# A two-layer decoder step on one core: the first and the last stage moved into the feed-forward blocks beside them

## The reference

```python
def rmsnorm(x, g):
    xf = x.astype(jnp.float32)
    y = xf * lax.rsqrt(jnp.mean(xf * xf, axis=-1, keepdims=True) + RMS_EPS)
    return y.astype(x.dtype) * g

def swiglu(h, w_in, w_out):
    gu = h @ w_in
    return (jax.nn.silu(gu[..., :D_FF]) * gu[..., D_FF:]) @ w_out
...
x += 0.5*SwiGLU(rms(x)); x += mixer(rms(x)); x += 0.5*SwiGLU(rms(x))
```

## Time and profile before

| what | value |
|---|---|
| median of 3 runs | 2402.17 us (2398.2 to 2403.61) |
| the profiled execution's own time | 2401.8 us |
| its span in the trace | 2400.0 us |
| PE busy | 2278.6 us (95%) |
| DVE, ACT, POOL busy | 1081.9, 737.5, 334.2 us |
| mean granted TensorE clock | 0.974 |

### The profile page before, as it was taken

One profiled execution on the slowest core, in us unless ns is written; L12 is line 12 of the kernel. 1 busy time (PEld: TensorE's weight loads), 2 busy tenths in 40 slices (PEclk: granted clock), 3 DMA queues, 4 the chain that ended last, 5 costly groups with the idle time before them and its releaser, 6 DMA issues. The chain is left out here.

```text
span 2400.0 us, 42964 instructions
## 1 busy us (share of the span) xinstructions
PE 2278.6 (95%) x17146; PEld 2057.5 (86%) x17146; DVE 1081.9 (45%) x1907; ACT 737.5 (31%) x1224; POOL 334.2 (14%) x422
## 2 busy tenths in 40 slices
PE   5999999996899999999999999999998889999997
PEld 5999999775764479999999999999665479999997
DVE  5442443223267644433434442444376735433433
ACT  2221332223146533322222221322255523322221
POOL 1000003100135321000012000003174320000002
PEclk8999999997999999999999999999999989999998
DMA  3332332224430022333232333332213022232331
GB/s 99 96 101 81 90 97 78 82 79 125 159 115 1 27 68 84 95 97 88 87 102 75 95 96 88 89 100 71 79 53 109 1 70 79 88 105 79 87 101 58
DMA packets 328119, 202.53 MB, mean 84 GB/s; under 512 B 11698, under 2 KB 307946, under 8 KB 327962
## 3 DMA queue, kind: packets, MB, share of 16 engines
q1 hardware_dynamic: 323866, 199.19, 27.9%
q10 hardware_dynamic: 4160, 2.10, 0.3%
HBM read 194.74 MB, written 10.70 MB: 86 GB/s over the span
## 5 line engine op out<-in xcount | busy, mean ns | idle before, releaser
L159 DVE TENSOR_TENSOR w_lo<-w_stage,w_hi 128x1024 fp32r<-128x1024 f32 (+1 forms) x268 | 356.4, 1330 | 827.1 <-ACT w_hi L152 827.0
L152 ACT ACTIVATE w_hi<-w_stage 128x1024 fp32r<-128x1024 f32 (+1 forms) x278 | 314.0, 1130 | 751.0 <-PE y_ps L166 344.2
L164 PE MATMUL gate_ps<-h_hi,w_hi 128*128 128x260 f32 x1408 | 402.3, 286 | 17.2 <-DVE h_lo L188 7.5
L165 PE MATMUL gate_ps<-h_lo,w_hi 128*128 128x260 f32 x1408 | 401.1, 285 | 0.0
L166 PE MATMUL gate_ps<-h_hi,w_lo 128*128 128x260 f32 x1408 | 400.3, 284 | 0.0
L164 PE MATMUL up_ps<-h_hi,w_hi 128*128 128x260 f32 x1408 | 398.8, 283 | 0.0
L164 PE MATMUL y_ps<-a_hi,w_hi 128*128 128x260 f32 x1408 | 398.5, 283 | 0.0
L165 PE MATMUL up_ps<-h_lo,w_hi 128*128 128x260 f32 x1408 | 398.1, 283 | 0.0
L165 PE MATMUL y_ps<-a_lo,w_hi 128*128 128x260 f32 x1408 | 398.0, 283 | 0.0
L166 PE MATMUL y_ps<-a_hi,w_lo 128*128 128x260 f32 x1408 | 397.9, 283 | 0.0
L166 PE MATMUL up_ps<-h_hi,w_lo 128*128 128x260 f32 x1408 | 397.4, 282 | 0.0
(11 more groups left out here) (420 smaller groups left out, 3142.4 us busy)
## 6 DMA issues: line engine op xcount, KB each, us to landing
w_stage<-w_ffn_in SPq DMA_DIRECT2D x176, 512.0 KB, 3.7
w_stage<-w_ffn_out SPq DMA_DIRECT2D x64, 704.0 KB, 4.5
w_stage<-w_nsa_in SPq DMA_DIRECT2D x20, 512.0 KB, 3.4
w_stage<-w_dsa_in SPq DMA_DIRECT2D x16, 512.0 KB, 3.6
w_stage<-w_nsa_out SPq DMA_DIRECT2D x8, 512.0 KB, 3.6
cmp_page<-cache_nsa_cmp SPq DMA_DIRECT2D x16, 256.0 KB, 4.3
w_stage<-w_dsa_out SPq DMA_DIRECT2D x8, 512.0 KB, 3.7
nsa_win_s<-state_nsa_win SPq DMA_DIRECT2D x1, 4080.0 KB
```

The lines of the kernel that those rows point to most:

```text
L152: act.activation(e.w_hi[slot][:, 0:cols], e.w_stage[slot][:, 0:cols], ACT.Copy).then_inc(e.hi_done, 1)
L159: dve.tensor_tensor(e.w_lo[slot][:, 0:cols], e.w_stage[slot][:, 0:cols], e.w_hi[slot][:, 0:cols].bitcast(F32), ALU.subtract).then_inc(e.lo ...
L164: pe.matmul(out, w_hi, x_hi, start=first, stop=False)
L165: pe.matmul(out, w_hi, x_lo, start=False, stop=False)
```

## The change

- `start_stage` and `final_stage` go. Two classes, `Start` and `Finish`, put their work into the streams of `ffn` 0 and `ffn` 3.
- **Start, loads**: the identity comes first, as the first 128 columns of the constants, then `x` in four loads of 128 tokens, each with its own semaphore, with the small loads between the second and third; the rest of the constants comes after weight unit 0.
- **Start, turning**: by token tile. Four transposes fill a bank with half a tile, DVE copies it into four chunks of `e.x` at once.
- **Start, norm**: ACT squares the token rows as they lie, 1024 elements each, and accumulates a sum for each token in a column (`start_sumsq`, 128 x 5). Root and reciprocal are taken on 128 x 5. DVE multiplies the identity by the factors (`rs_diag`), and in the middle of unit 1 PE multiplies it by ones, which spreads the factors over all partitions; DVE copies them to `e.rs`.
- **Start, rest**: `h_hi` no longer waits for a block's end, the two casts (`ident_b`, `causal_b`) move behind the `w_lo` of unit 2, POOL does only three memsets.
- **Finish**: ACT makes `y` as `x` times the gain, without the norm factor, as each chunk is ready (`y_of`), between the weight splits of `ffn` 3. A root of `eps` ahead of the last chunk makes the table of roots current. After the last product PE turns 7 of 8 chunks of three token tiles, then takes the sums of squares as columns (128 x 5; the last chunk's squares come from DVE as a second operand), then turns the rest. DVE and ACT copy one half of each tile each, and multiply by the factor of the token there.

The diff, cut to its core:

```diff
+class Start:
+    def sync(self, sp):
...
+        sp.dma_start(e.const[:, 0:P], e.c_const[:, 0:P]).then_inc(e.ident_landed, 16)
+        for t in range(2):
+            sp.dma_start(rows[:, t, :], xp[:, t, :]).then_inc(e.x_landed[t], 16)
+        sp.dma_start(rows[0:TS, 4, :], e.x_sample.rearrange("b s d -> (b s) d")).then_inc(e.start_loaded, 16)
+        sp.dma_start(gains[0:6 * KC, :], e.norm_g.rearrange("l s (k p) -> (l s k) p", p=P)).then_inc(e.start_loaded, 16)
+        sp.dma_start(gains[6 * KC:7 * KC, :], e.final_norm_g.rearrange("(k p) -> k p", p=P)).then_inc(e.start_loaded, 16)
+        for t in range(2, 4):
+            sp.dma_start(rows[:, t, :], xp[:, t, :]).then_inc(e.x_landed[t], 16)
+        load_units(e, sp, 0, 1)
+        sp.dma_start(e.const[:, P:], e.c_const[:, P:]).then_inc(e.const_landed, 16)
+        sp.dma_start(e.table[:, :], e.page_table.rearrange("(o b) n -> o (b n)", o=1)).then_inc(e.const_landed, 16)
+        load_units(e, sp, 1, 2)
...
+    def turns(self, pe):
+        e, rows = self.e, self.rows
+        pe.wait_ge(e.ident_landed, 16)
+        for t in range(4):
+            pe.wait_ge(e.x_landed[t], 16)
+            for i in (2 * t, 2 * t + 1):
+                if i >= 4:
+                    pe.wait_ge(e.x_done, i - 3)
+                for k in range(4):
+                    at = (i % 2 * 4 + k) * P
+                    m = pe.transpose(self.bank(i)[:, k * P:(k + 1) * P], rows[:, t, at:at + P], e.ident[:, :])
+                m.then_inc(e.turned, 1)
...
+    def spread_rs(self, pe):
+        e = self.e
+        pe.wait_ge(e.const_landed, 32)
+        pe.wait_ge(e.rs_spread, 2)
+        for t in range(4):
+            pe.matmul(self.y_ps[1][:, 0, t * P:(t + 1) * P], e.ones[:, :], self.spread[:, t * P:(t + 1) * P], start=True, stop=True)
...
+    def scalar(self, act):
+        e, rows = self.e, self.rows
+
+        def square(t, n, done):
+            act.wait_ge(e.start_squared, done)
+            act.activation(self.squares[0:n, :], rows[0:n, t, :], ACT.Square, accum_out=self.sumsq[0:n, t:t + 1])\
+               .then_inc(e.start_squared, 1)
+        for t in range(4):
+            act.wait_ge(e.x_landed[t], 16)
+            square(t, P, t + 1)
+        act.wait_ge(e.start_loaded, 48)
+        square(4, TS, 5)
+        act.wait_ge(e.turned, 5)
+        act.activation(e.x[:, :, TP:T], self.up_ps[:, 1, 0:KC * TS].rearrange("p (k t) -> p k t", k=KC), ACT.Copy)\
+           .then_inc(e.sample_turned, 1)
+        split_hi(e, act, 0, 0, e.cols_of(0))
...
+        for k in range(KC):
+            act.wait_ge(e.x_done, 7 + k // 4)
+            h_hi_of(e, act, 0, k)
...
+    def spread_factors(self, dve):
+        e = self.e
+        dve.wait_ge(e.rms_done, 1)
+        dve.reciprocal(e.rs_col[:, :], e.rms_col[:, :]).then_inc(e.rs_spread, 1)
+        dve.wait_ge(e.rs_spread, 1)
+        for t in range(4):
+            dve.tensor_scalar(self.spread[:, t * P:(t + 1) * P], e.ident[:, :], e.rs_col[:, t:t + 1], None, ALU.mult)
+        dve.tensor_scalar(self.spread[0:TS, TP:T], e.ident[0:TS, 0:TS], e.rs_col[0:TS, 4:5], None, ALU.mult).then_inc(e.rs_spread, 1)
+
+    def keep_rs(self, dve):
+        e = self.e
+        dve.wait_ge(e.stat_ready, 1)
+        dve.tensor_copy(e.rs[:, 0:TP], self.y_ps[1][:, 0, 0:TP])
+        dve.tensor_copy(e.rs[:, TP:T], self.y_ps[1][:, 1, 0:TS]).then_inc(e.rs_done, 1)
...
+class Finish:
...
+    def y_of(self, act, k):
+        e = self.e
+        act.wait_ge(e.x_done, self.x_base + k + 1)
+        act.activation(self.y[:, k, :], e.x[:, k, :], ACT.Copy, scale=e.gain[:, 6 * KC + k:6 * KC + k + 1]).then_inc(e.y_done, 1)
...
+    def turns(self, pe):
...
+        turn(0, 0, KC - 1)
+        turn(1, 0, KC - 1)
+        pe.wait_ge(e.x_done, self.x_base + KC - 1)
+        turn(2, 0, KC - 1)
+        pe.wait_ge(e.sum_done, self.sums)
+        pe.wait_ge(e.last_squared, 2)
+        for t in range(NT):
+            for i, part in enumerate((e.sumsq, self.last_sq)):
+                m = pe.matmul(self.stat[:, t:t + 1], part[:, t * P:(t + 1) * P], e.ones[:, 0:1], start=i == 0, stop=i == 1)
+        m.then_inc(e.stat_ready, 1)
+        for t in range(3):
+            turn(t, KC - 1, KC)
+        turn(3, 0, 4)
+        pe.wait_ge(e.rms_done, self.n + 1)
+        turn(3, 4, KC)
+        pe.wait_ge(e.row_copied, 1)
+        pe.wait_ge(e.row_scaled, 1)
+        turn(4, 0, KC)
...
@@ in ffn
             def statistics():
                 pe.wait_ge(e.sum_done, sums)
-                if at_start:
-                    pe.wait_ge(e.start_added, KC)
...
             for half in range(2):
                 b = in0[half]
                 F = f0 + half * FH
                 split_lo(e, dve, b + 1, 0, KC * P)
-                if half == 0 and at_start:
-                    for k in range(KC):
...
+                if half == 0 and begin:
+                    begin.spread_factors(dve)
                 split_lo(e, dve, b + 2, 0, KC * P)
                 if half == 0:
-                    dve.wait_ge(e.rms_done, e.norm_n + 1)
-                    dve.reciprocal(e.rs[:, :], e.rms[:, :]).then_inc(e.rs_done, 1)
+                    if begin:
+                        begin.casts(dve)
+                        begin.keep_rs(dve)
...
-def start_stage(e, sum_squares):
...
-def final_stage(e):
...
```

More of the change, by code:

```diff
@@ L340, in out_unit @@
                 m.then_inc(e.unit_used, 1)
+            if begin:
+                begin.turns(pe)
             for half in range(2):
                 for side in range(2):
-                    in_unit(in0[half], 0, f0 + half * FH, side, half == 0)
-                    if half == 0 and side == at_start:
+                    in_unit(in0[half], 0, f0 + half * FH, side, half == 0,
+                            begin.spread_rs if begin and half == 0 and side == 1 else None)
+                    if half == 0 and side == 0 and not begin:
                         statistics()
@@ L371, in silu_of @@
                 act.activation(silu_t[:, :, :], gate_t[:, :, :], ACT.Silu).then_inc(e.silu_done, 1)
-            build_h_act(e, act, norm)
+            if begin:
+                begin.scalar(act)
+            else:
+                build_h_act(e, act, norm)
             for half in range(2):
@@ L377, in _ @@
                 split_hi(e, act, b + 1, 0, KC * P)
+                if half == 0 and begin:
+                    begin.root(act)
                 split_hi(e, act, b + 2, 0, KC * P)
-                if half == 0:
+                if half == 0 and not begin:
                     act.wait_ge(e.stat_ready, e.norm_n + 1)
@@ L503, in _ @@
                 x_of(half, o + KC, 1, 0, KC - 1)
+            if finish:
+                finish.square(dve)
+                finish.vector(dve)
+        if begin:
+            e.x_rows += KC
     e.built = AHEAD_H if follows else 0
```

283 lines of the change are left out of this document (141 added, 142 removed).

## The result

The changed kernel takes 2372.68 us, median of 4 runs (2369.83 to 2373.74), where the kernel before took 2401.23 us in the same rounds (4 runs, 2398.2 to 2403.61). The ratio is 0.988 with a 95% interval of 0.9863 to 0.9897: 28.6 us less. The forecast was 2370 in a range of 2362 to 2378. The profiled execution of after took 2373.74 us, with a span of 2371.9 us and a mean granted clock of 0.978 (before 0.974).

What follows compares the result with a forecast made beforehand. PE standing still at the two ends was taken as the question. From 2400.0 us, 20.3 at the start and 11.9 at the end leave 2367.8 of span, 2369.6 with 1.8 outside, so 2370; range 2362 to 2378.

Steps and rivals of the forecast that it cites:

- Last tile and ACT's chain: Start: last x tile lands at 10.3 us; squares, copy and weight splits behind it bring PE's first product at 16.3.
- turning and copying ends by 13, beside this chain: Start: the last tile's 8 transposes at 0.10 to 0.14 us and two copies of 0.75 end by 13.
- Unit 0: First unit of products: paced as before by h_lo and a mean clock of 0.79, 7.16 us, ending at 23.4.
- Factors: Start: norm factors done between 23.3 and 27.1 us, taken as 24.6, scalings 0.25 each, hidden before spreading at 27.1.
- Spreading, and unit 2: Start: spreading the factors takes PE 1.3 us (1.0 to 2.1); gate_t done at 30.1, unit 2 without a stop after 30.65.
- Rival 3: Before unit 2: factors come late, PE waits 1 to 2 us and may fall to half clock; up to 2374.5, chance 0.10.
- Start in all: Start: PE begins 7.2 us earlier and 13.1 us come from the removed stop and half clock; 20.3 us gained.
- The middle: Between the two ends: not touched by the change, since all its streams read as before.
- The fifth rival: Middle mixers: start shifted by 20 us raises lost clock by more than 32 us; 2405 and more, chance 0.01.
- The tail: After the last product at 2374.49: scaling moved under products, stores bound the rest, end at 2388.1; gain 11.9 us.
- Rival 1: Tail: runs at half clock, transposes 0.9 us longer and one-column products 2.6 longer; 2373.5, chance 0.14.
- Rival 2: Start loads: each awaited tile pays the 3.9 us fixed part, last landing up to 11.7 later; 2382, chance 0.05.

Runs made afterwards that it cites:

- e11_again: The changed kernel run again with no edit; 2369.11 us, ratio 0.9871 against the kernel before.
- e10_fill_both: The changed kernel plus unread filler products on PE at the program's start and in both sample attentions; 2360.28 us, ratio 0.9837 against the kernel before.
- e5: The changed kernel with the constants ahead of x again and x in one load; 2376.31 us, ratio 0.9896 against the kernel before.
- e6: The changed kernel with seven scaled chunks made only behind the last chunk of x; 2377.91 us, ratio 0.9904 against the kernel before.
- e8: The changed kernel plus unread filler products in PE's waits in both sample attentions; 2364.33 us, ratio 0.9849 against the kernel before.
- e13: The changed kernel run again with no edit, in another batch; 2371.22 us, ratio 0.9873 against the kernel before.
- e7_no_preload: The changed kernel without the small root that brings ACT's table in early; 2369.72 us, ratio 0.9866 against the kernel before.

## Why the prediction was right, point by point

- **Last tile and ACT's chain.** The last tile's square began at 10.12 us, for a landing predicted at 10.3. The chain was forecast to bring the first product at 16.3; it came at 16.16 (15.93 and 16.43 in the other two profiles of this kernel). But in the profile of after it was not ACT's chain that ended last. `w_hi` was ready at 13.56, and `w_lo` waited until 14.12 for DVE, whose copies followed PE's turning. The step "turning and copying ends by 13, beside this chain" failed by 1.0 us: the prediction took 0.10 to 0.14 us for a transpose, and 32 of them ran at 0.21 to 0.23 each from the first landing on. In the other two profiles the step nearly held and ACT's chain ended last, as forecast: the second sixteen transposes were fast, the copies ended at 13.28 and 13.15, and `w_hi` was ready at 13.75 and 14.25. Two chains of nearly the same length covered for each other, so that 16.3 came out within 0.4 us in all three is in part luck. The row of `e11_again`, to be held against the 3.43 us for the same sixteen in after:

```profile
9.97 1.97 PE L284 MATMUL y_ps<-const,x_rows 128*128 128x128 f32 x16
```

- **Unit 0** took 7.1 us at clock 0.76, for 7.16 at 0.79 before: as forecast, the same. The reason given was half wrong. `h_lo` does not pace it: its eight passes took 5.45 us here for 6.43 before, and unit 0 was no shorter. PE was busy all through (7.11 of 7.11 us, 7.12 of 7.16 before), so the clock alone paced it; at full clock in `e10_fill_both` it took 5.8 us.
- **Factors.** Ready at 22.98, for 24.6 forecast and under the lower bound of 23.3. DVE came to the reciprocal at 21.77 and not at 23.1, since `h_lo` was faster; the scalings took 0.22 us each (0.88 for four) for the 0.25 taken. None of this is on the path. Spreading began at 27.09, as forecast.
- **Spreading, and unit 2.** Spreading held PE from 27.09 to 28.39, the 1.3 us taken. `gate_t` was done at 29.99 (30.1 forecast) and unit 2 came at 30.7 (30.65) at full clock. Rival 3, factors that come late, did not occur in the three profiles of this kernel.
- **Start in all:** 20.3 us forecast, 20.3 measured at the first mixer, and 20.6 and 20.1 in the repetitions. The agreement to the digit is luck, as the repetitions show. No run undoes the path of the norm factors alone; its 13.1 us are read from the profiles.
- **The middle** was forecast to stay. It took 3.3 us more in this profile, 0.1 less and 2.8 more in the repetitions up to `dsa_z_ps`, and 0.0, 2.4 and 1.6 less behind it. That differs between executions of one kernel and is no fixed cost of the change. The fifth rival named the right place, low clock in the middle mixers. Its reason, the phase, does not decide it, and it never came near the 32 us that it needed.
- **The tail** was forecast 25.5 to 13.6 and is 14.4; 13.2 and 14.7 in the repetitions. Turning took 2.3 us for 2.1 and ran at full clock, and the one-column products 2.14 for 2.6. The first store went out 5.8 us behind the last product in all three (6.0 forecast). From there to the end, forecast 7.6, it was 8.6, 7.4 and 8.9: the mis-sized term is the stores', by 1.0 us in after. In after the fifth store was issued 3.9 us after the first, 3.0 in `e11_again` (rows below), and the data paused for part of a microsecond in between. Rival 1, the tail at half clock, showed in none of the three: the granted clock is 1.00 over the first 4.56 us of each tail.

```profile
2357.17 2.90 SPq L459 DMA_DIRECT2D y_prompt<-y_rows  x4
2360.16 1.18 SPq L461 DMA_DIRECT2D y_sample<-y_rows  x1
```

- **Sum.** Forecast 2367.8 of span, measured 2371.9, which is 3.3 us in the middle and 0.8 in the tail. That the time of all runs, 2372.68, is 2.7 us from the 2370 forecast says little by itself, as single runs of this kernel lie 7 us apart. The three profiles of this kernel have 2371.9, 2364.6 and 2370.3.
- **Rival 2**, a fixed cost for every tile, was rightly small for tiles that are queued: tiles landed 3.7 to 6.4 us behind their issue, overlapped, and the last began to be used at 10.12. It is not nothing for what stands ahead, as the 2.8 us for two loads and 528 KB show (1.4 of them bytes, 0.8 SP's issuing). The fit that the prediction takes from the Trainium skill is given there for DMAs that GpSimd issues; SP issues these, so they are no test of it.

What the estimate could not have was the draw: a program of 2400 us with some ten stretches at low clock has its runs 7 us apart, more than any term on which the forecast could have been better.

## What to carry to other kernels

A first or last stage of its own, in which one engine after another works, is worth folding into the neighbour that keeps PE busy, and its gain can be summed from the rows of before to within a microsecond: here 20.3 and 11 to 12 us of 2400. Factors for each token belong in columns of 128 x 5 (0.18 us for the reciprocal, where the 128 x 520 one took 3.40), and spread or applied in copies that are made anyway. Before a loss in an untouched part is put down to a change, run the same kernel again and compare the same 20 us: anchors on both sides of every piece tell a cost from a draw.

## What the runs showed of the hardware

- The same instructions at the same place had their stretch at half clock for some 3 us in one execution and for some 14 in the next (0.91 and 0.66 over 20 us), and the piece around it was 3 us longer. Some 70 products in PE's pauses removed the stretch of the second attention altogether (2 profiles with them, 12 without); together with 40 in the first the kernel was 4.8 us faster.
- The granted clock reads 1.00 for 5 to 14 us of after (the row below), and yet the transposes there took 0.21 to 0.23 us each, as at half clock; in the tail, at 1.00 as well, the same 128 x 128 transposes took 0.11 (2.29 us for 21). With 36 products ahead of them (`e10_fill_both`) they took about 0.14. So at the start of this program the row of the clock does not tell the speed, and the duration of an instruction does.

```profile
5.00:14.00 9.00, 8.24 (x41) 7.53 (x41) 5.55 (x9) 7.17 (x13) 0.00 (x0) 1.00 0.96 321
```

- In the ten profiles with the new turning and no fillers at the start, the first sixteen transposes took 3.6 to 4.0 us. The second sixteen took 1.96 to 2.08 us in five of them (`e5`, `e6`, `e8`, `e11`, `e13`) and 3.43 to 3.67 in the other five, with nothing but transposes on PE until then.

- The ACT table load of `e7_no_preload` ran ahead of the wait of the root that needs it. ACT stood there for 2.9 us in all, 1.28 for the load and 1.65 idle, and the preload was worth nothing.
- The same four stores and one took 7.4 to 8.9 us from first issue to the end in three executions of one kernel.
